# Hybrid trunk on one core: order of the first norm, of mixer 0's loads, of mixer 1's first products and of the last piece

## The reference, cut to what matters

```python
for l in range(2):
    shift, scale, gate = split(silu(c) @ w_ada[l, 0] + b_ada[l, 0])
    h = rms(x, norm_gain[l, 0]) * (1 + scale) + shift
    x = x + gate * hybrid_mixer(h)       # z = h @ w_in: latents for 8 attention heads (columns 0:416),
                                         # two groups of 512 for a gated linear recurrence; then @ w_out
    shift, scale, gate = split(silu(c) @ w_ada[l, 1] + b_ada[l, 1])
    h = rms(x, norm_gain[l, 1]) * (1 + scale) + shift
    x = x + gate * (swiglu(h) if l == 0 else top2_of_8_experts(h))   # widths 2816 and 3584
```

## Time and profile before

| | |
|---|---|
| time, median of 3 runs | 1471.91 us (1471.38 to 1472.97) |
| the profiled execution | 1475.58 us, span 1474.0 us, mean granted clock 0.985 |
| PE busy | 1419.8 us, 96% |
| DVE busy | 1242.4 us, 84% |
| ACT busy | 904.0 us, 61% |
| DMA | 484.40 MB, mean 329 GB/s |

### The profile page before, as it was taken

The page is one execution under the profiler, slowest core; times in us unless marked ns, Lnnn a source line. Parts: engine busy times, 40 slices in busy tenths (PEclk is TensorE's granted clock), DMA queues, the critical chain, the costliest instruction groups (busy, mean ns, idle before and its releaser), DMA issues.

```text
span 1474.0 us, 18431 instructions
## 1 busy us (share of the span) xinstructions
PE 1419.8 (96%) x6949; PEld 1158.2 (79%) x6949; DVE 1242.4 (84%) x1060; ACT 904.0 (61%) x802; POOL 45.7 (3%) x79
## 2 busy tenths in 40 slices
PE   4989799999989999999999999999999999999998
PEld 1775799997775788888888888888888888888885
DVE  3479687775877799999899999999999989999997
ACT  2073443343073677777777777777777777777775
POOL 1000000000000000000000000000000000000011
PEclk8999899999999899999999999999999999999998
DMA  9965659875935699999899999999999999999993
GB/s 348 360 272 195 247 182 378 292 294 204 351 115 190 247 374 371 348 397 395 333 395 393 333 397 396 383 347 393 388 339 397 394 335 395 393 332 397 396 369 80
DMA packets 195481, 484.40 MB, mean 329 GB/s; under 512 B 8854, under 2 KB 31604, under 8 KB 191348
## 3 DMA queue, kind: packets, MB, share of 16 engines
q1 hardware_dynamic: 186736, 451.17, 82.0%
q0 software_dynamic: 6480, 32.52, 5.9%
q10 hardware_dynamic: 2228, 0.22, 0.1%
HBM read 473.39 MB, written 10.49 MB: 328 GB/s over the span
## 4 chain that ended last, share of the span: by engine, by line
PE 91%; DVE 6%; ACT 1%; issue 1%; DMA 0%; ACTq 0%; DVEq 0%
PE ps L993 21%; PE ps L995 21%; PE ps L994 20%; PE ps L679 4%; PE ps L860 3%; PE ps L859 3%; PE ps L858 3%; PE ps L825 2%; PE ps L672 2%; PE ps L1032 2%; PE ps L867 1%; PE ps L868 1%; PE ps L866 1%; PE ps L606 1%; DVE tokens L1363 1%
## 5 line engine op out<-in xcount | busy, mean ns | idle before, releaser
L1867 DVE TENSOR_TENSOR split_r<-arena,split_r 128x2048 fp32r<-128x2048 f32 x339 | 770.5, 2289 | 71.9 <-ACT split_r L1294 70.1
L1294 ACT ACTIVATE split_r<-arena 128x2048 fp32r<-128x2048 f32 x338 | 648.0, 1917 | 131.9 <-PE ps L995 131.9
L993 PE MATMUL ps<-split_r,tokens_r 128*128 128x512 f32 x1280 | 505.6, 395 | 1.5 <-DVE split_r L1867 1.5
L995 PE MATMUL ps<-split_r,tokens_r 128*128 128x512 f32 x1280 | 499.4, 390 | 0.0
L994 PE MATMUL ps<-split_r,tokens_r 128*128 128x512 f32 x1280 | 498.3, 389 | 0.0
L995 PEld LDWEIGHTS ps<-split_r,tokens_r 128*128 128x128 f32 x1280 | 240.2, 188 | 51.3
L993 PEld LDWEIGHTS ps<-split_r,tokens_r 128*128 128x128 f32 x1280 | 240.4, 188 | 49.9 <-DVE split_r L1867 2.4
L994 PEld LDWEIGHTS ps<-split_r,tokens_r 128*128 128x128 f32 x1280 | 240.6, 188 | 48.0
L858 PE MATMUL ps<-tokens_r,split_r 128*128 128x256 f32 x352 | 99.2, 282 | 5.0 <-DVE hT_r L1732 5.0
L860 PE MATMUL ps<-tokens_r,split_r 128*128 128x256 f32 x352 | 100.1, 284 | 0.0
L859 PE MATMUL ps<-hT_r,split_r 128*128 128x256 f32 x352 | 100.0, 284 | 0.0
(11 more groups left out here) (333 smaller groups left out, 1350.2 us busy)
## 6 DMA issues: line engine op xcount, KB each, us to landing
arena<-in_moe_w_gate SPq DMA_DIRECT2D x57, 2048.0 KB, 9.8
arena<-in_moe_w_up SPq DMA_DIRECT2D x57, 2048.0 KB, 10.2
arena<-in_moe_w_down SPq DMA_DIRECT2D x56, 2048.0 KB, 9.4
arena<-in_w_ada POOLq DMA_DIRECT2D x10, 1536.0 KB, 10.5
arena<-in_w_ada SPq DMA_DIRECT2D x14, 1024.0 KB, 12.7
arena<-in_ffn_w_gate SPq DMA_DIRECT2D x11, 1024.0 KB, 7.5
arena<-in_ffn_w_up SPq DMA_DIRECT2D x11, 1024.0 KB, 13.1
arena<-in_ffn_w_down SPq DMA_DIRECT2D x11, 1024.0 KB, 14.7
```

The costliest lines, as they stand in the source:

```text
L993: mm(out_, xh, h, start=first, stop=False, skip_group_check=True)
L995: return mm(out_, xl, h, start=False, stop=last_, skip_group_check=True)
L1294: A(wh[:, j % SPLITS, :], piece_half(j), ACT.Copy).then_inc(sem("w_hi"), 1)
L1867: v.tensor_tensor(wl[:, j % SPLITS, :], piece_half(j), wh[:, j % SPLITS, :].bitcast(F32), ALU.subtract).then_inc(sem("w_lo"), 1)
```

## The change

1. **First norm earlier.** ACT squares x and takes the two roots before the sine and the two constant copies; DVE runs both `normalise` calls ahead of the setup of the recurrence and of the angles. A further Sqrt on one element stands behind the copies.
2. **SP's wait for the small rows** stands before the fourth load, not the second.
3. **Mixer 0's order of loads.** w_in piece 0, all the gate pieces (seven: six of one k, one of two), then w_in pieces 1 to 3 between the ada pieces of sub-layer 1; seven of these eight waits go, and w_out comes behind them, in cells 9, 10 and 12.
4. **DVE's ada steps.** Six before the latents are copied (the gate broadcast between the fifth and the sixth), one behind the updates of each tile.
5. **Dense head by tiles.** The first dense piece is split at the end of mixer 0 (ACT behind the second root, DVE behind the first update of the second round); norm 1 is transposed, evacuated and split by tile.
6. **Mixer 1.** All latent products of tile 0 first, then the wait for tile 1, then the loop with tile 1's latents; column sums of ada 3 in one go behind `turn_qk(1)`, their modulation on DVE before the second row maximum.
7. **Experts.** The output slots are computed before the second half of `hl`, and the low halves behind them. In the last half piece of a pass the result's first half is finished before the second; DVE scales by halves.

```diff
-        fills += [("win", 0, i, SPLIT0 + i, []) for i in range(4)]
-        fills += [("gate", 0, i, None, [("ada_row", 6)] if i == 3 else []) for i in range(5)]
+        fills += [("win", 0, 0, SPLIT0, [])]
+        fills += [("gate", 0, i, None, []) for i in range(7)]
+        fills += [("win", 0, 1, SPLIT0 + 1, [])]
+        fills += [("ada", 1, 0, TOKENS, [("ada_row", 4)]), ("ada", 1, 1, 0, [])]
+        fills += [("win", 0, 2, SPLIT0 + 2, [])]
+        fills += [("ada", 1, 2, 1, []), ("ada", 1, 3, 2, [])]
+        fills += [("win", 0, 3, SPLIT0 + 3, [])]
+        fills += [("ada", 1, 4, 5, [("ada_row", 6)])]
         fills += [("bias", 0, 0, None, [])]
+        fills += [("ada", 1, 5, 6, [])]
         fills += [("small", 0, 0, None, [("wbd_zero", 1)])]
-        fills += [("ada", 1, k, c, w) for k, (c, w) in enumerate((
-            (TOKENS, []), (0, []), (1, []), (2, []), (12, [("rec_ps", 2)])))]
-        fills += [("wout", 0, i, SPLIT0 + i, []) for i in range(3)]
-        fills += [("ada", 1, k, c, w) for k, c, w in (
-            (5, 0, [("ada_step", 8 + 2)]), (6, 1, [("ada_step", 8 + 3)]), (7, 2, [("ada_step", 8 + 4)]))]
+        fills += [("ada", 1, 6, 0, [("ada_step", 8 + 2)]), ("ada", 1, 7, 1, [("ada_step", 8 + 3)])]
+        fills += [("wout", 0, i, SPLIT0 + (0, 1, 3)[i], [("rec_ps", 2)] if i == 0 else []) for i in range(3)]
...
-                ([("o_ps", 2), ("rec", 1)], [], [("wout_done", 5)])[c]) for c in range(CHUNKS)]
+                ([("o_ps", 2), ("rec", 1)], [("ss_o", 2)], [("wout_done", 5)])[c]) for c in range(CHUNKS)]
...
-                if n == 1:
+                if n == 3:
                     sp.wait_ge(sem("rowsA_in"), 16 * 12)
...
+                if l == 1:
+                    for i in range(4):
+                        parts.append(part(place(wait_fill(pe, "win", l, i), 2 * IN_COLS), 0, 2, IN_COLS))
+                    for k in range(KD):
+                        latents(0, k)
+                    tile_ready(2, 1)
                 for i in range(4):
...
-                    for t in range(NT):
+                    for t in range(l, NT):
...
                 turn_qk(1)
+                if l == 1:
+                    ada_reduce(place(TOKENS, 3 * D), 2 * KD, 2, step["ada", 3, KD - 1])
...
-                norm_transposes(1, lambda: ada_reduce(place(TOKENS, 3 * D), 2 * KD, 0, step["ada", 1, KD - 1]))
+                tile_transposes(1, 0)
+                pe.wait_ge(sem("x_new"), 1)
+                ada_reduce(place(TOKENS, 3 * D), 2 * KD, 0, step["ada", 1, KD - 1])
+                tile_transposes(1, 1)
...
+                        order = [(f, n) for f in range(EFT // 2) for n in range(2)]
+                        if j == HP - 1:
+                            order = [(f, n) for n in range(2) for f in range(EFT // 2)]
+                        for f, n in order:
+                                ff = half * EFT // 2 + f
...
+                                if j == HP - 1 and (f, n) == (EFT // 2 - 1, 0):
+                                    last.then_inc(sem("down_ps"), 1)
...
+            act.wait_ge(sem("x_in"), 16)
+            for t in range(NT):
+                A(xn[:, t, :], x[:, t, :], ACT.Square, accum_out=st[:, t:t + 1]).then_inc(sem("ss_n"), 1)
             act.wait_ge(sem("cols_in"), 1)
...
+            root(1, 0)
+            root(1, 1)
             act.wait_ge(sem("ang"), 1)
...
+            A(mark[:, 8:9], ones[:, 0:1], ACT.Sqrt)
...
-                if l == 1:
+                if l == 0:
+                    act.wait_ge(sem("ffn_g0_in"), 16)
+                    act.wait_ge(sem("wout_done"), 4)
+                    A(wh[:, 0, :], unit("g", 0), ACT.Copy).then_inc(sem("f_hi"), 1)
+                else:
...
+                sum_squares(1)
                 act.wait_ge(sem("y_out"), 16)
+                for t in range(NT):
+                    evacuate_tile(1, t)
+                    for half, ready in enumerate(("hT_act", "hT_dve")):
+                        act.wait_ge(sem(ready), tile_count(1, t))
+                        A(hh[:, 4 * half:4 * half + 4, t * P:(t + 1) * P], hT[:, 4 * half:4 * half + 4, t * P:(t + 1) * P],
+                          ACT.Copy).then_inc(sem("hh"), 1)
...
-            for i in range(4):
+            for i in (3, 0, 1, 2):
...
-                    steps("ada", 1, range(3))
+                    steps("ada", 1, range(5))
                     gate_broadcast(0, 2)
+                    steps("ada", 1, (5,))
...
-                if l == 0:
-                    steps("ada", 1, (3, 4))
                 for t in range(NT):
                     for half in range(2):
                         update(t, half, 0, rs[:, t:t + 1])
                     if l == 0:
-                        steps("ada", 1, (5 + t,))
+                        steps("ada", 1, (6 + t,))
...
-                if l == 0:
-                    steps("ada", 1, (7,))
                 update(0, 0, 1, rs[:, 4:5])
                 if l == 1:
                     low(0, 0)
+                else:
+                    dve.wait_ge(sem("f_hi"), 1)
+                    v.tensor_tensor(wl[:, 0, :], unit("g", 0), wh[:, 0, :].bitcast(F32), ALU.subtract)\
+                        .then_inc(sem("f_lo"), 1)
...
+                modulation(1)
+                evacuate_tile(1, 0)
+                low_tokens(0)
+                evacuate_tile(1, 1)
+                low_tokens(1)
...
-                        dve.wait_ge(sem("w_used"), (p + 1) * HP + SPLITS)
                         dve.wait_ge(sem("swT"), p + 1)
-                        v.scalar_tensor_tensor(out=ynat, in0=bank2(4), scalar=w_slot, in1=gate_row, op0=ALU.mult,
-                                               op1=ALU.mult).then_inc(sem("y_sb"), 1)
+                        for n in range(2):
+                            if n:
+                                dve.wait_ge(sem("w_used"), (p + 1) * HP + SPLITS)
+                            else:
+                                dve.wait_ge(sem("down_ps"), p + 2 * NT)
+                            cols = slice(512 * n, 512 * n + 512)
+                            last = v.scalar_tensor_tensor(out=ynat[:, cols], in0=ps[:, 4 + n, :], scalar=w_slot,
+                                                          in1=gate_row[:, cols], op0=ALU.mult, op1=ALU.mult)
+                        last.then_inc(sem("y_sb"), 1)
```

145 lines of the change are left out of this document (61 added, 84 removed).

## The result

The changed kernel takes 1462.71 us in the median (1460.04 to 1464.38, 4 runs), the kernel before, run beside it, 1472.44 (1471.38 to 1474.06, 4 runs): a ratio of 0.9931, 95% interval 0.9913 to 0.995, or 9.7 us less: clear of noise, and under 1%. In a second measurement on another chip it was 1462.51 against 1473.38, ratio 0.9921 (0.9907 to 0.9934). The forecast was 1456.4 with a range of 1453 to 1461.5: the direction was right, and more than a third of the gain forecast did not come (9.7 of 15.5 us).

What follows compares the result with a forecast made beforehand. PE was taken as full for 1.16 ms that no edit touches; terms elsewhere sum to -15.5 us, taking the profiled 1475.6 to 1460.1, less 3.7 to the median: 1456.4 us, range 1453 to 1461.5.

Steps and rivals of the forecast that it cites:

- The front: First norm and load order, 0 to 37 us: PE starts mixer 0's latents at 32.9 instead of 37.0, -4.1 us.
- After, three 1 MB loads are queued before that wait ... so the gap closes: Front: 4.2 MB with x cover the stream's gap at 8 to 13 us, taken as 2.7 us won.
- Rival 2: Front: small rows wait for the big loads, land near 15.5, PE starts near 36; total 1459.5, chance 15%.
- That stays: Front: the 4.3 us from the last ada product's end to the first latent product remain unchanged.
- hidden by the wait for piece 7 with 1.2 us to spare: Front: ACT's extra table switches end near 27.4, covered by the wait for the last ada piece.
- margin of 1.2 us: Mixer 0: second w_in piece lands at 44.5, PE wants it at 45.7; a start before 31.7 would be given back.
- Rival 3: Mixer 0 starves if the stream averages below 300 GB/s; it moved 339 or more per slice; above 1472, chance 2%.
- End of mixer 0 and dense head: 128 to 166 us: ada steps leave DVE's chain (net -4.65), column sums run at full clock (-3.1); -7.3 us in all.
- The dense stage: PE is its only bound, so gains made ahead of it are kept; 0 us change inside it.
- Mixer 1: First tile's latents fill PE's wait for the second tile, -1.75 us; ada 3 column sums moved, -1.0 us.
- The experts' entry: Slots computed while DVE waits for the gather, so PE no longer waits for the fourth low half: -1.4 us.
- Last piece: End of the experts' passes: the early signal for scaling by halves finds DVE busy in two low halves, +0.1 us.

Runs made afterwards that it cites:

- x_after: The changed kernel again, unchanged, on another chip: 1462.51 us, ratio to the kernel before 0.9921.
- x_nowait: The changed kernel without SP's wait for the small rows: 1461.17 us (1 run).
- x_dvecopy: x_nowait's edit, x_latestep's edit and DVE instead of ACT copying the first norm's summed rows, on the changed kernel: 1460.83 us, ratio 0.9908.
- x_clump: x_dvecopy with the first norm's sixteen transposes behind the sixth ada piece, not the fourth: 1459.89 us, ratio to before 0.9898.
- x_best: The same kernel as x_clump, run once more beside the changed kernel: 1459.51 us, ratio to before 0.9898.
- x_win: x_best with the second w_in piece queued behind four of the seven gate loads, not all seven: 1459.12 us, ratio to before 0.9907.
- x_nosteps: The changed kernel with the last two ada steps of mixer 0's end left out (pieces missing from the sum): 1462.26 us (1 run).
- x_undo1: The changed kernel with both mixer 1 edits undone (latents wait for both tiles, ada 3 sums in two blocks): 1464.75 us, ratio to before 0.9941.
- x_latestep: The changed kernel with the dense stage's first ada 2 step moved behind the next down unit: 1460.08 us, ratio to before 0.9906.
- x_undo2: The changed kernel with the slots' work back behind the low halves and the result scaled in one piece: 1461.73 us, ratio to before 0.9924.
- x_yfirst: The changed kernel with DVE scaling the expert's result ahead of the low half of the weights in every pass: 1464.96 us, ratio to before 0.9935.

## Why the prediction was wrong, point by point

**The front (-4.1 forecast, -0.9 measured, -1.7 in x_after): the step that failed** is "After, three 1 MB loads are queued before that wait ... so the gap closes". I took the rows' landing at 10.2 as given; beside a full stream it is 14.3 (14.8 in x_nowait), so SP's wait opened the gap again, and the last piece's product started at 29.9 and ended at 31.0, not at 28.6: 2.4 of the 3.2 us that are missing. Rival 2 had this outcome, with 15.5 and a start near 36. Its mechanism, rows that wait until the loads ahead of them have drained, x_nowait refutes. What holds is what the Trainium skill, Trainium Kernel Development and Optimization, section Key Constraints, says: queues of several issuers run on the same engines and interleave. The trace agrees: in x_nowait the rows landed at 14.8 while 378 GB/s went by. The prediction called that sharing the mechanism of rival 2, which it is not. I had priced it by a load of 4.71 us, beside traffic that soon ended, against 3.3; beside a continuous stream the same load took 8.6.

The other 0.8 us are the clock of one execution: from the last ada product to the first latent product it was 5.1 us and not 4.3, by the column products at the lower level (1.87 us for 1.06). In x_after, the same kernel, it was 4.3 again. "That stays" took full clock there without a reason; whether the moved transposes make the lower level more likely is not shown.

One more statement was wrong and cost nothing here: "hidden by the wait for piece 7 with 1.2 us to spare". In the changed kernel the last piece came so late that ACT's copy followed it by 0.07 us; once the stream runs through, ACT's chain ends 1.3 us too late, as x_nowait and x_dvecopy show.

And the whole term could not have been had. With the gap and the copy mended (x_clump, x_best) PE starts at 33.8 to 34.1, 1.2 to 2.3 us earlier than in the two profiles of the changed kernel, and waits 1.7 to 2.0 us for the second w_in piece; the dense stage starts 0.8 to 1.4 us earlier. I had put that piece at 44.5, it came at 47.2 to 47.8, and PE wants it 12.8 us after its start: what it wins ahead of 34.4 to 35.0 it waits for again. The changed kernel itself had that wait in x_after (0.76 us, started at 35.3). In x_win another order of the loads only moved the wait. The "margin of 1.2 us" was the true bound of this term, and it was worked out from a stream that is 3 us ahead of the real one. (Rival 3's "339 or more in every slice of 4 us" holds to 56 us only; slices between 56 and 63 us of the trace before have 289 to 322 GB/s.)

**End of mixer 0 and dense head (-7.3 forecast, -7.5 measured): right**, term by term: the chain, 0.19 us for the copy, sums at full clock. Measured from the head of DVE's chain (the root's reciprocal at 128.02 before, 127.04 after, 127.20 in x_after) to the first dense product it is 7.4 us less in both profiles. x_nosteps adds that PE's projections are now the bound there.

**The dense stage (0 forecast, +2.06 measured): a wrong step.** "PE is the only bound of the dense stage, so it is kept". The kernel before had a margin of some 0.4 to 1.0 us that I did not look for: DVE idled 4.65 us on a load, and PE begins to wait when that is above 5.0 to 5.6. The load took 8.7 us instead of 6.7, and 1.3 us were gone. It is issued at the same distance from the stage's start (52.2 and 52.3 us) and the change touches nothing near it; over ten profiles of kernels with this step in its place the idle varied between 4.65 and 7.08. But 4.65 is the only profile of the kernel before and the lowest of the ten, so it is not excluded that the change has a part in it. What sets the load's duration stays open. Some 0.3 more is the clock (0.64 in the first 5 us of the stage, 0.70 before; 0.50 in x_after, where the stretch lost 3.6 us), and 0.4 is left open.

**Mixer 1 (-1.75 and -1.0 forecast, -2.37 and -1.00 measured): right.** x_undo1 takes back 2.24 in the median. The 0.6 above the forecast is the clock ahead of it: the gate sums took 2.62 us for 3.66, the transposes ahead of them 1.97 for 1.09. The eight latent products were put at 0.70 us each, the figure of the lower clock; they took 0.36, and 2.9 us for all eight still fill the wait.

**The experts' entry (-1.4 forecast, -1.5 with what stands before it): right in size by luck.** 1.33 us come ahead of the gather's end: 1.7 from the gather at full clock (3.81 for 5.53), 0.6 from the products between it and the logits, 0.2 ahead of the logits, less 1.2 for the logits at a lower clock (5.34 us for 4.18). No edit touches these. In x_after this stretch lost 1.45. The edit itself gave 0.2. Its worth goes with that clock: from the gather's end to the last scaling it is 963.3 us before, 961.6 to 961.7 in the four profiles of the new order where the gather took 5.1 to 6.6 us (x_clump, x_after, x_latestep, x_nowait), and 963.0 to 963.1 in the eight where it took 3.8 (the changed kernel and x_best among them). With a slow gather DVE has its slots ready and the edit wins 1.7 against the one profile of before; with a fast one DVE's low halves are late in either order, and it wins 0.3 against x_undo2. My sum read one profile, in which the gather was slow.

**Last piece (+0.1 forecast, +0.1 measured): right.** From the first scaling to the spread it is 1.53 us for 1.41, and x_yfirst confirms the reason.

**The scale.** The profiled execution of before stood 3.7 us above its median, that of after 1.7. I subtracted 3.7 from the sum. That makes 2.0 of the miss of 6.3; in the later measurements the median of before was 1472.7 to 1474.7, so the 1471.9 of three runs was on its low side. The other 4.3 are 3.2 at the front and 2.1 in the dense stage, less 1.0 of small gains above the forecast; in x_after the same total is made up of other parts.

## What to carry to other kernels

A load's duration read in a stretch where the stream stands still need not hold once the change fills that stretch: ask what the small loads on the other queue take beside a full stream, and do not make the large ones wait for them. Where a term pays into a later stage, follow each load with the new start time until the stage's end; the smallest margin caps the term, however it was won. And a chain at the head of a stage that runs now at one clock, now at the other, decides what an edit there is worth: read it in more than one profile.

## What the runs showed that was not expected

The time of one and the same kernel varies by some 4 us between the executions beside one another (the changed kernel) and by up to 7.5 (the kernel before), and the profiles show where: over all kernels with the same products there, the gather of the experts' entry took 3.81 to 6.73 us, the logits 3.71 to 5.34, and the first 5 us of the dense stage ran at a mean granted clock of 0.50 to 0.71. The largest is the last spread, eight products behind 2.9 us of idle time, here in the changed kernel and in x_after:

```profile
1452.27 6.70 PE L988 MATMUL ps<-hT,F_r 128*128 128x512 f32 x8 [2.93 <-DVE hT L1947]
...
1455.30 3.69 PE L988 MATMUL ps<-hT,F_r 128*128 128x512 f32 x8 [2.93 <-DVE hT L1947]
```

From its start to the end of the span it is 10.5 us in one and 7.6 in the other, 2.9 us of total time that no edit made. All four stand behind an idle PE, and the full level of 2.4 GHz came back earlier or later from one execution to the next. A row load of 0.8 KB took 4.7 us beside 2 MB of traffic that ended at 8.5 us, and 8.6 us beside 4.2 MB. And in x_yfirst a wait of PE for weights shows in its rows with 0.3 us and in those of the weight loads with 0.7, and 0.59 was lost each time.
